# A third home for the gathered V rows, and the second group's exponentials earlier, in a one-core decoder layer

## What is computed

```python
z = rmsnorm(x) @ w_in                       # -> rq, rk, rv, rg (retention), mq, mk, mv (attention)
# retention: 4 heads of 128, chunks of 128, with a state per sequence
s_new = decay * s + (k * k_dec).T @ v
out   = (q @ k.T * decay_in) @ v + (q * q_dec) @ s
# MoBA attention, 8 heads of 64: 3 best past blocks of 256 keys and the own block
gate  = q . mean(k of a block);  p = softmax(scale * q @ k_chosen.T);  o = p @ v_chosen
mix   = concat(norm(out) * gain * silu(rg), o);   h = x + mix @ w_out
# 32 experts, each token uses 4
u = rmsnorm(h) @ w_gu[e] + b_gu[e]
y = h + sum_e gate_e * (swiglu(u) @ w_dn[e] + b_dn[e]);   out = rmsnorm(y) * g
```

## Time and profile before

| | |
|---|---|
| median of three executions | 1317.76 us (1315.08 to 1320.0) |
| the profiled execution | 1313.23 us, its span 1311.3 us |
| PE busy | 1222.4 us, 93% |
| PE weight load | 515.3 us, 39% |
| DVE / ACT / POOL busy | 387.0 / 232.3 / 117.6 us |
| DMA | 500.64 MB, mean 382 GB/s |
| chain that ended last | PE 59%, DMA 25%, DVE 9%, issue 5% |

### The profile page before, as it was taken

How to read it: one execution, slowest core, us unless ns; L and a number is a source line. 1 busy time by engine, 2 the same in 40 slices (tenths; PEclk the granted TensorE clock), 3 DMA queues, 4 the chain that set the end, 5 groups by cost and what they waited for, 6 DMA issues and landing times.

```text
span 1311.3 us, 17401 instructions
## 1 busy us (share of the span) xinstructions
PE 1222.4 (93%) x7250; PEld 515.3 (39%) x7250; DVE 387.0 (30%) x551; ACT 232.3 (18%) x528; POOL 117.6 (9%) x117
## 2 busy tenths in 40 slices
PE   7999887658999999999999999999999999999996
PEld 3455443323553443434434343343434343343431
DVE  5999962205232211111211112211111112111113
ACT  3021141201421111101112011111201011211102
POOL 2222335263100000000000000000000000000000
PEclk8999998778999999999999999999999999999999
DMA  9999857873889999999999999999999999999994
GB/s 344 387 345 369 319 168 243 304 257 136 328 329 414 430 428 427 429 428 429 428 428 429 428 428 429 428 429 427 429 429 428 430 427 430 428 428 429 426 428 191
DMA packets 56316, 500.64 MB, mean 382 GB/s; under 512 B 6329, under 2 KB 6609, under 8 KB 27601
## 3 DMA queue, kind: packets, MB, share of 16 engines
q1 hardware_dynamic: 41840, 430.55, 78.4%
q0 software_dynamic: 14432, 69.47, 14.5%
HBM read 495.29 MB, written 4.72 MB: 381 GB/s over the span
## 4 chain that ended last, share of the span: by engine, by line
PE 59%; DMA 25%; DVE 9%; issue 5%; ACT 2%; POOL 1%; another core or an unknown queue 0%; SPq 0%; DVEq 0%; POOLq 0%; ACTq 0%
PE psum L904 22%; DMA arena<-w_gate_up 21%; PE psum L935 12%; DVE arena L1379 6%; PE psum L854 4%; PE psum L836 3%; DMA arena<-w_down 3%; PE psum L574 2%; PE psum L488 2%; PE psum L866 2%; PE psum L682 2%; PE psum L414 1%; PE psum L873 1%; PE psum L842 1%; POOL arena L1845 1%
## 5 line engine op out<-in xcount | busy, mean ns | idle before, releaser
L904 PE MATMUL psum<-arena 128*64 128x512 f32 x1920 | 422.7, 594 | 15.1 <-DMA arena<-w_gate_up 15.1
L904 PEld LDWEIGHTS psum<-arena 128*64 128x64 f32 x1920 | 134.9, 137 | 299.3 <-issue 264.6
L1699 DVE TENSOR_SCALAR arena<-psum 128x512 f32<-128x512 f32 x32 | 22.1, 692 | 682.2 <-PE psum L904 642.9
L935 PE MATMUL psum<-arena 128*64 128x512 f32 x960 | 212.6, 595 | 0.0
L1052 ACT ACTIVATE arena<-psum 64x512 f32<-64x512 f32 (+3 forms) x185 | 94.0, 510 | 406.1 <-PE psum L935 170.7
L1379 DVE STREAM_TRANSPOSE arena<-arena 128x2048 f32<-128x2048 f32 x32 | 121.6, 3946 | 2.7 <-PE psum L474 2.4
L935 PEld LDWEIGHTS psum<-arena 128*64 128x64 f32 x960 | 66.4, 137 | 124.1 <-issue 122.3
L488 PE MATMUL psum<-arena 128*128 128x512 f32 x224 | 107.2, 617 | 0.5 <-issue 0.4
L1270 ACT ACTIVATE arena<-arena 128x512 f32<-128x512 f32 x30 | 18.9, 631 | 418.8 <-DVE arena L1699 418.8
L1052 ACT ACTIVATE arena<-psum,arena 128x128 f32<-128x128 f32 (+2 forms) x182 | 53.8, 398 | 179.2 <-PE psum L488 124.6
L836 PE MATMUL psum<-arena 128*128 128x128 f32 x512 | 77.2, 294 | 0.0
(11 more groups left out here) (224 smaller groups left out, 733.0 us busy)
## 6 DMA issues: line engine op xcount, KB each, us to landing
arena<-w_gate_up SPq DMA_DIRECT2D x128, 2048.0 KB, 29.7
arena<-w_down SPq DMA_DIRECT2D x64, 2048.0 KB, 33.4
arena<-w_in SPq DMA_DIRECT2D x7, 2048.0 KB, 21.2
arena<-w_out SPq DMA_DIRECT2D x2, 2048.0 KB, 9.7
out<-arena SPq DMA_DIRECT2D x4, 512.0 KB, 2.6
out<-arena POOLq DMA_DIRECT2D x1, 2048.0 KB, 13.0
arena<-x_prompt SPq DMA_DIRECT2D x2, 512.0 KB, 4.7
arena<-cache_v,arena POOLq DMA_INDIRECT x64
```

The lines of the kernel that those rows point to most:

```text
L904: last = mm(psum[64 * g:64 * (g + 1), b, :], xt[:, 2 * kk + m, lhs], gate_slot[slot][:, m, c:c + 512], start=False, stop=kk == 3 and m == ...
L935: last = mm(psum[64 * g:64 * (g + 1), 2, :], at_sb[:, m, SLOTS * q:SLOTS * (q + 1)], down_slot[slot][:, m, 512 * g:512 * (g + 1)], start=q ...
```

## The change

V gets a third home of 2 MB. Set n goes to home n mod 3. Home 0 and home 1 are the two of before; the third is the place at word 12288 for sets 2 and 5, and place 0 (free after projection block 6) for sets 8, 11 and 14. Set n now waits for v_used = n-2, and set 2 for nothing; set 8 waits for block 6 too. To free the place at 12288, `s_prompt` and `pt_prompt` change places, so the load of the retention state waits for the prompt's products (`prompt_o`) and no longer only for its transposes. The ring's slots are renamed: turn 0 uses the V home of set 13, turn 1 the one of set 14, turn 2 the one of set 15, and each is loaded when its set has been used. Separately, `probabilities(1)` moves up on ACT, and the reciprocal of group 1 moves up on DVE, out of `evacuate_own(1)`.

```diff
-PLACE = (0, 6, 7, 4, 5, 3, 1, 2)
+PLACE = (7, 0, 6, 4, 5, 3, 1, 2)
...
-        pt_prompt = at(DN, 24, P)
-        s_prompt = at(12288, 24, P)
+        s_prompt = at(DN, 24, P)
+        pt_prompt = at(12288, 24, P)
...
-        v_raw = at(KV, 2, 4, 2 * 512)
+        def v_raw(n):
+            home = KV + 4096 * (n % 3) if n % 3 < 2 else 12288 if n < 6 else 0
+            return at(home, 4, 2 * 512)
...
 # PE, values(v)
-                    pe.wait_ge(v_in[x], 64 * (v + 1))
+                    n = 2 * v + x
+                    pe.wait_ge(v_in[n % 3], 64 * (n // 3 + 1))
...
 # ACT
             evacuate_pt(2)
+            probabilities(1)
             for u in range(0, 6, 2):
                 evacuate(pt_prompt[:, 4 * u:4 * u + 4, :].rearrange("p b t -> p (b t)"))
...
             evacuate(qd_t.rearrange("p h t -> p (h t)"))
-            probabilities(1)
             evacuate_pt(3)
...
 # DVE
-            def evacuate_own(g):
+            def own_reciprocal(g):
                 dve.wait_ge(own_probs, g + 1)
                 w = sm[:, g, :]
                 link(v.reduce_sum(w[:, 49:50], w[:, 40:49], axis=AXX))
                 v.reciprocal(w[:, 50:51], w[:, 49:50]).then_inc(o_recip, 1)
+
+            def evacuate_own(g):
+                w = sm[:, g, :]
                 V.wait_full(dve)
...
             V.emptied(v.tensor_copy(mix_t[:, 6:8, 0:LP],
                                     psum[:, V.bank(), :].rearrange("p (c w) -> p c w", c=2)))
+            own_reciprocal(1)
...
 # POOL, v_set(n)
-                else:
-                    pool.wait_ge(v_used, n - 1)
+                elif n > 2:
+                    pool.wait_ge(v_used, n - 2)
+                if n == 8:
+                    pool.wait_ge(*mark["block6"])
...
 # SP
-            wait_all(sp, mark["prompt_t"])
+            wait_all(sp, mark["prompt_o"])
             sp.dma_start(state.rearrange("p s h v -> p (s h) v"),
...
-            sp.wait_ge(*mark["block6"])
-            load_turn(0)
             sp.wait_ge(kdec_ready, 1)
...
+            sp.wait_ge(v_used, V_SETS - 2)
+            load_turn(0)
             sp.wait_ge(*mark["pt7"])
...
+            sp.wait_ge(v_used, V_SETS - 1)
+            load_turn(1)
             sp.wait_ge(v_used, V_SETS)
-            load_turn(1)
             load_turn(2)
```

More of the change, by code:

```diff
@@ L342, in build_kernel @@
         win_in = [sem(f"win_in{i}") for i in range(3)]
-        v_in = [sem(f"v_in{i}") for i in range(2)]
+        v_in = [sem(f"v_in{i}") for i in range(3)]
         k_in = [sem(f"k_in{i}") for i in range(4)]
@@ L575, in values @@
                                       pt_sb[:, v % 2, j * P + s:(j + 1) * P:4],
-                                      v_raw[:, x, s, 512 * r:512 * (r + 1)], start=False,
+                                      v_raw(n)[:, s, 512 * r:512 * (r + 1)], start=False,
                                       stop=q == 3 and j == 3, skip_group_check=True)
@@ L1478, in _ @@
             rotate(rot_q, mark["z3"])
+            own_reciprocal(0)
             evacuate_own(0)
@@ L1840, in v_set @@
                     pool.wait_ge(k_trans, K_UNITS - 2 + 2 * n)
-                else:
-                    pool.wait_ge(v_used, n - 1)
+                elif n > 2:
+                    pool.wait_ge(v_used, n - 2)
+                if n == 8:
+                    pool.wait_ge(*mark["block6"])
                 for s in range(4):
                     row = v_rows[:, 4 * (n // 8) + s, n % 8:n % 8 + 1]
-                    pool.indirect_dma_start(out=v_raw[:, n % 2, s, :], out_offset=None, in_=cv,
+                    pool.indirect_dma_start(out=v_raw(n)[:, s, :], out_offset=None, in_=cv,
                                             in_offset=bass.IndirectOffsetOnAxis(ap=row, axis=0),
-                                            bounds_check=n_phys * 64 - 1).then_inc(v_in[n % 2], 16)
+                                            bounds_check=n_phys * 64 - 1).then_inc(v_in[n % 3], 16)
             def v_block(h):
```

## The result

The changed kernel takes 1309.92 us (median of 11 executions; the fastest 1303.12) against 1317.76 us for the kernel before on the same chip (11 executions, 1313.88 to 1321.06). The ratio is 0.993 with a 95% interval of 0.9914 to 0.9946: 7.8 us less than the median predicted from, where 20 were forecast. One execution of the eleven, 1774.58 us at a granted clock of 0.649 where the others have 0.97, is left out of the ratio. The profiled execution took 1311.33 us, its span 1309.5 us. The two profiled executions, 1313.23 before and 1311.33 after, differ by 1.9 us only.

What follows compares the result with a forecast made beforehand. The experts' weight stream bounds it, 928.6 us behind the first expert matmul. Ahead of it 9.2 - 2 + 3.4 + 1.3 + 0.3 + 2.2 + 5.2 = 19.6, say 20 us gained: 1298 us on the median, range 1286 to 1307.

Steps and rivals of the forecast that it cites:

- (a): `values(1)`: sets 2 and 3 land earlier, so its second half ends at 195.5 instead of 204.7 us; gain 9.2 us.
- (b): Small sample matmuls (L457) beside POOL's issue of set 6: cost between 0 and 4.4 us, taken as 2.
- (c): `probabilities(1)` moved up on ACT: gain 4.2 - 0.8 = 3.4 us, plus 1.3 from `values(3)` no longer following an idle stretch.
- (d): Reciprocal moved up on DVE, ahead of L554 and L567: gain 0.3 us, plus 2.2 from an unnamed stall, bounds 0 and 5.5.
- (e): `values(5)`: set 10 goes out ten microseconds earlier, so only set 11 is issued at that point; gain 5.2 us.
- (f): From L714 on: nothing waits for V, turns 1 and 2 go out behind the loads of x; no gain in the sum.
- sample part L457 over 6 us: Sign of being wrong: the 64 sample matmuls of L457, 1.95 us at 211.76, lasting more than 6 us.
- The rival of small losses beside gathers: If (b) costs 4.4 us, set 5 lands 2 late, transposes lose about 4: some 9 lost, 1307 us; chance 0.14.
- list of waits for V: PE's waits for V in the kernel before: 1.79 us before 192.57, 6.53 before 201.06, 1.30 before 277.28.
- The warm case: Rival: PE's stalls go and the clock stays up, 10 us more, 30 in all, 1288 us; chance 0.20.
- The block of 928.6 us: From the first expert matmul (382.69 us) to the end, set by the stream of weights; claimed to keep its length.

Runs made afterwards that it cites:

- fourth chip: Changed kernel with the gathers of sets 1, 2 and 6 held back: 1295.13 us, against 1312.28 for the changed kernel; with the early memset of `y` too, 1285.67.
- fifth chip: Third home without the moves of `probabilities(1)` and the reciprocal, against the kernel before: 1309.86 us, before 1318.37 (0.9944).
- third chip: Third home without the moves of `probabilities(1)` and the reciprocal, against the changed kernel: 1281.19 us, changed 1271.61, kernel before 1299.79.
- second chip: Changed kernel with the memset of `y` ahead of the state's store, against the changed kernel: 1266.22 us, changed 1273.70, kernel before 1299.83.

## Why the prediction missed

The sum of 19.6 us, term by term, against the recorded traces:

| step | forecast | recorded pair |
|---|---|---|
| (a) `values(1)` | +9.2 | +9.4 |
| (b) small matmuls beside gathers | -2 | -13.9 |
| (c), (d) moves, reciprocal, stall | +7.2 | +0.5 |
| (e) set 11 | +5.2 | +4.2 |
| (f) the rest up to `values(7)` | 0 | +11.5 |
| (f) behind `values(7)` | 0 | -9.7 |
| sum | 19.6 | 2.0 |

**(a) was right** in what it claimed: both waits for V gone, and block 6 of tile 1 ahead of its old place. (The prediction's last section names the wait in the second half of `values(1)` both as one that falls to about 0 and as one that is left; it fell to 0.)

**(b) is the step that failed.** Its cost was bounded at 4.4 us, from one place, and taken as 2. It came at two places and with a second part each time. The prediction let set 2 go out "behind set 1, about 155 us" and priced only set 6. But at 155 the other sample part is running: it went from 6.3 to 10.0 us. The second went from 1.95 to 6.6. And after each the granted clock was down: 0.87 instead of 1.00 over the block of 32, which took 16.09 us instead of 14.00, and 0.56 instead of 1.00 over `values(2)`, 6.39 us instead of 3.67. Full speed is 2.4 GHz, and at 0.56 most of `values(2)` ran at 1.2. Together with 0.7 us of later start that is 6.6 + 7.3 = 13.9. The fourth chip shows the cause by taking it away: 17 us back, with the gaps beside set 1 among them. The prediction had "sample part L457 over 6 us" among its signs of being wrong, and that sign came. The rival of small losses beside gathers named the mechanism, at 9 us lost and 1307. Of its three terms only the first, the second sample part at its full cost, came; the sample part beside set 2 and the slow clock behind both are not in it. That its time is within 3 us of the measured one is luck.

**(c) and (d) failed too, on chips with gaps.** The prediction booked the 4.23 us of exponentials as gained, less 0.8, and a part of the stall ahead of L554, 2.2 us of at most 5.5. The fifth chip shows that beside the third home the moves add nothing there: ACT and DVE stall on something that the trace calls "remote", and L571 starts at the same time with or without the moves (259.7 and 259.8). The prediction had said that it could not name this stall. It should have asked whether the exponentials in (c) lie ahead of the same kind of stall. On chips without gaps both steps work: 9.6 us on the third chip for 7.2 forecast.

**(e) was right**: 4.2 us for 5.2, with the only wait for V that is left in the recorded trace, 3.52 us before the second half of `values(5)`. The Trainium skill's formula in "DMA: Bandwidth & Descriptors", section "Anatomy of one DMA — SWDGE (gpsimd) path", would have added 2.3 us. The trace does not agree: from the last issue of set 11 to its landing it has 5.28 us, where the formula gives an estimate of 3.2.

```profile
270.02 5.28 DMA arena<-cache_v,arena
```

The prediction's list of waits for V leaves out the longest in the kernel before, ahead of the first half of `values(5)`:

```profile
272.33 3.65 PE L574 MATMUL psum<-arena 128*32 128x512 f32 x16 [7.20 <-DMA arena<-cache_v,arena]
```

Its sum did not need it, since (e) counts from one issue to the next.

**(f) missed two effects of opposite sign.** Up to the end of `values(7)` 11.5 us are gained that I had at nothing: L723 has fewer gaps (5.8 us instead of 9.2), a wait of 2.84 us for DVE ahead of the next L737 is gone, and `values(6)`, L737 and `values(7)` run at a faster clock (3.67 us for `values(7)`, 5.83 before). The prediction gave no reason why these should change or stay. Behind it 9.7 are given back. I had written that turns 1 and 2 go out "behind the loads of x" and looked only at the turns. The loads of x themselves wait for a memset that stands behind the state's store on POOL; with V earlier, that was next. Moving the memset gives 7.5 us on the second chip, without gaps, and 9.5 on the fourth, with gaps, there on top of the held gathers.

**The warm case** (1288, a gain of 30) is what chips without gaps do: 26 to 28 us, with the stall gone as that rival had it. Its argument was that slow pieces stand behind idle ones. The rows agree, `values(2)` at 3.67 or 6.39 us after a whole or a broken sample part, and so does the Trainium skill, "TensorE: Matmul & The Clock Gate", section "What's actually happening". But whether the idle goes was a matter of the chip, and no row of the profile before could tell that.

**The block of 928.6 us** behind the first expert matmul held (928.9), and with it the frame of the argument: what moves that matmul moves the end.

What stays open: why some chips have the gaps, how a gather makes them, and what the stall is. Gaps and stall belong to the same chips, and the gaps need a gather beside small matmuls. Neither changes the packets that the queues show for instructions: the kernel before has 32 on one queue and 12 on the other on both kinds of chip, the changed kernel 32 and 11.

## What to carry to other kernels

When a freed buffer lets transfers go out earlier, list what every engine does in the stretch where they are now issued, and price each such stretch from a row where the two already meet; here that row, 6.3 us against 1.95, stood in the profile and was used for one place of two. After a gain, look for what is released by an instruction behind a store or a wait on an idle engine's list: a memset there cost 7.5 to 9.5 us. And compare only within a chip: the same change was worth 0.7% on one and 2.1% on another.

## What the runs showed of the hardware

- Two kinds of chip, for the same program: 1300 us and 1318 us, with ratios that agree within a kind to 0.3%. On the slower kind 64 matmuls of 128x128 with 32 rows last 6 to 10 us beside POOL's indirect DMAs (gaps of 0.3 to 1.1 us in the recorded traces) and 1.93 to 1.96 without them, even with a DMA share of 1.04; on the faster kind 1.93 to 1.96 beside them too.
- Matmuls of 128x512 beside the same DMAs show no such gaps: 32 take 14.00 us with eight gathers issued beside them.
- The block (L492) behind a sample part that lasts 6.1 to 6.3 us, with the gathers of set 1 beside it only, still takes 14.00 us. Behind one of 9.0 to 10.4 us, with those of set 2 beside it too, it takes 16.09, 16.45 and 16.67 us.
- On the slower kind PE waits 5.4 to 6.5 us for stalled ACT and DVE just ahead of L571 (or of L558, where the reciprocal is not moved) in every kernel; on the faster kind it waits 0.9 us there.
- An indirect DMA takes POOL 1.00 us to issue, and 1.15 to 1.94 us in the stretch where DVE executes TENSOR_TENSOR of 128x768 to 128x2048 (190 to 202 us in the changed kernel).
